# Attention by pairs of query tiles, with values and turned probabilities split into high and low parts

## The reference

```python
def block(args):                       # one tile of 128 queries
    qn, qp, i = args
    s = (jnp.einsum('bqhd,bkhd->bhqk', qn, k_nope)
         + jnp.einsum('bqhr,bkr->bhqk', qp, k_pe)).astype(jnp.float32) * scale
    s = jnp.where(causal, s, -jnp.inf)
    p = jax.nn.softmax(s, axis=-1).astype(v.dtype)
    return jnp.einsum('bhqk,bkhd->bqhd', p, v)
...
o_mla = mla_attention(...) * jax.nn.silu(g_mla)
o_s5 = s5_layer(...) * jax.nn.silu(g_s5)
return jnp.concatenate([o_mla, o_s5], axis=-1) @ w_out
```

## Time and profile before

| | us |
|---|---|
| median of 3 runs | 891.39 |
| the profiled execution | 895.35 |
| its span, from the first to the last instruction | 893.3 |
| TensorE busy (4360 matmuls) | 852.8, 95% |
| TensorE weight loads | 691.8, 77% |
| VectorE busy | 590.0, 66% |
| ScalarE busy | 326.9, 37% |
| GpSimd busy | 248.1, 28% |
| mean granted TensorE clock | 0.986 |

### The profile page before, as it was taken

How to read it: one execution, slowest core, us unless ns; L and a number is a source line. 1 busy time by engine, 2 the same in 40 slices (tenths; PEclk the granted TensorE clock), 3 DMA queues, 4 the chain that set the end, 5 groups by cost and what they waited for, 6 DMA issues and landing times.

```text
span 893.3 us, 12333 instructions
## 1 busy us (share of the span) xinstructions
PE 852.8 (95%) x4360; PEld 691.8 (77%) x4360; DVE 590.0 (66%) x961; ACT 326.9 (37%) x626; POOL 248.1 (28%) x251
## 2 busy tenths in 40 slices
PE   7999999999999999999998999999799999999995
PEld 5899777756677777787875888888588888888884
DVE  6988688557687775637871443488986667544543
ACT  6251514654333434412222645045243446111210
POOL 2000001415211111506656231005753013332243
PEclk9999999999999999999998899999999999999998
DMA  9101164220000111032223110236334322111111
GB/s 335 35 20 30 48 118 96 50 74 1 1 2 1 39 34 48 1 105 108 95 95 118 47 48 1 83 94 191 123 102 140 105 74 103 38 61 48 48 59 59
DMA packets 40685, 64.21 MB, mean 72 GB/s; under 512 B 8256, under 2 KB 21824, under 8 KB 40608
## 3 DMA queue, kind: packets, MB, share of 16 engines
q1 hardware_dynamic: 40624, 63.42, 23.2%
HBM read 52.33 MB, written 9.44 MB: 69 GB/s over the span
## 4 chain that ended last, share of the span: by engine, by line
PE 72%; DVE 17%; ACT 3%; DMA 3%; issue 2%; SPq 1%; POOL 1%; DVEq 0%; ACTq 0%; POOLq 0%
PE psum L1876 39%; PE psum L2177 14%; PE psum L2100 6%; PE psum L1963 6%; PE psum L1885 6%; PE psum L1911 1%; DVE vg_lo L1748 1%; DVE probT L696 1%; DMA wgs_raw<-even_w_in_dram 1%; DVE x_hi_raw L1779 1%; DVE x_lo_raw L1780 1%; DMA xT_raw<-x_cols_dram 1%; DMA ln_gb<-ln_b_dram 1%; DVE qTt L1617 1%; ACT xT_hi L1117 1%
## 5 line engine op out<-in xcount | busy, mean ns | idle before, releaser
L2177 PE MATMUL psum<-vg_hi,x1T_hi 128*128 128x512 f32 x208 | 82.0, 394 | 4.9 <-DVE vg_lo L1748 4.2
L2177 PE MATMUL psum<-vg_hi,x1T_lo 128*128 128x512 f32 x208 | 81.7, 393 | 0.0
L2177 PE MATMUL psum<-vg_lo,x1T_hi 128*128 128x512 f32 x208 | 81.6, 392 | 0.0
L2100 PEld LDWEIGHTS psum<-V,probT 128*128 128x128 f32 x576 | 69.3, 192 | 12.4 <-issue 8.4
L1209 ACT ACTIVATE prob<-psum,negmax 128x128 f32<-128x128 f32 (+7 forms) x64 | 47.4, 741 | 82.0 <-DVE negmax L1623 74.4
L2100 PE MATMUL psum<-V,probT 128*128 128x64 f32 x576 | 74.5, 275 | 0.5 <-DVE rot L1684 0.3
L1963 PE MATMUL psum<-kT,qTt 96*128 96x512 f32 (+3 forms) x192 | 72.5, 487 | 1.2 <-DVE YT L713 1.2
L1623 DVE TENSOR_REDUCE negmax<-psum 128x1 f32<-128x128 f32 (+7 forms) x64 | 48.5, 758 | 28.2 <-PE psum L1967 26.7
L696 DVE COPY probT<-psum 128x512 f32<-128x512 f32 (+3 forms) x64 | 37.8, 591 | 22.4 <-PE psum L1885 20.7
L2177 PEld LDWEIGHTS psum<-vg_hi,x1T_hi 128*128 128x128 f32 x208 | 39.3, 189 | 15.3 <-DVE vg_lo L1748 6.2
L1876 PE MATMUL psum<-x1T_lo,wqk_hi 128*128 128x512 f32 x128 | 50.8, 397 | 0.0
(11 more groups left out here) (393 smaller groups left out, 2087.5 us busy)
## 6 DMA issues: line engine op xcount, KB each, us to landing
vg_piece<-odd_w_in_dram SPq DMA_DIRECT2D x60, 256.0 KB, 3.3
wqk_raw<-odd_w_in_dram SPq DMA_DIRECT2D x8, 512.0 KB, 5.3
x_res<-x_dram SPq DMA_DIRECT2D x8, 512.0 KB, 4.0
x_scratch<-zn SPq DMA_DIRECT2D x8, 512.0 KB, 2.9
w_out_raw<-odd_w_out_dram SPq DMA_DIRECT2D x4, 1024.0 KB, 5.0
V<-x_scratch SPq DMA_DIRECT2D x8, 512.0 KB, 4.4
out_dram<-SG SPq DMA_DIRECT2D x8, 512.0 KB, 2.9
xT_raw<-x_cols_dram SPq DMA_DIRECT2D x7, 512.0 KB, 7.6
```

The lines of the kernel that those rows point to most:

```text
L2100: mm = pe.matmul(bank("o", i)[:, h * VD:(h + 1) * VD], lhsT, rhs, start=(k == 0), stop=(k == len(pairs) - 1))
L2177: mm = pe.matmul(bank(*job), lhsT, rhs, start=(k == 0 and j == 0 and product not in ADDS_TO), stop=(k == 3 and j == len(pairs) - 1), skip_ ...
```

## The change

- The 64 heads run in pairs of tiles: four pairs (2p, 2p+1), in each the 8 heads, and for each head the even and then the odd tile. Product "av" m belongs to the two heads 2m and 2m + 1.
- Values of a key block stand as four groups of 64 columns: for an even head high and low, for an odd head low and high (fp32r). ScalarE writes two copies, GpSimd subtracts.
- Turned probabilities go into one of three cells, each with a high and a low part (fp32r) for both tiles. ScalarE copies every group (high), VectorE subtracts this from the same bank (low).
- "av": the values (128 columns: high and low of one head) are stationary, the probabilities of both tiles (256 columns) move past them, once high and once low. In the last key block of a pair only the odd tile takes part. The output comes turned. Bank 7 holds two heads; when both are done, ScalarE copies it ("o" to `o_parts`), and two matmuls with a shifted identity ("ob") add the lower half onto the upper one or the reverse, in the same bank.
- The gate is scaled by the inverse row sums (`gate_scaled`), turned ("gT"), copied by ScalarE, and multiplied with the output by VectorE in two halves (`output_gated`). "OT" is gone.
- Queries of tiles 0 and 1 and the GLU product are done ahead of the first scores; the sigmoid is one function on ScalarE; the S5 gate is multiplied in four operations.
- w_out's rows are loaded and split after the last queries; `wqk`'s first load stands behind the last "o", ahead of the norm's rows, which wait for the last "ob"; its two splits stand behind the norm's tiles 2 and 3 on GpSimd.

The diff, cut to what the text speaks of (memory offsets and semaphore names left out):

```diff
...
+            yield "q", 1
-            yield "q", 1
+                yield "glu", n
+            yield "qT", 1
+            for n in range(4):
-            for n in range(4):
-                yield "glu", n
...
-        heads = [(i, h) for i in range(NT) for h in range(H)]
+        heads = [(2 * p + t, h) for p in range(NT // 2) for h in range(H) for t in range(2)]
...
+                p, r = divmod(n, 16)
-                if h < 2 and i + 1 < NT:
-                    yield "qT", (i + 1, h)
-                if h in (2, 3) and i + 2 < NT:
-                    yield "q", (i + 2, h - 2)
+                if p and r in (1, 2):
+                    yield "qT", (2 * p + r - 1, 1)
+                if p < 3 and r in (10, 11):
+                    yield "qT", (2 * p + r - 8, 0)
+                if p < 3 and r in ((3, 5, 6, 7) if p else (0, 1, 2, 3)):
+                    nth = ((3, 5, 6, 7) if p else (0, 1, 2, 3)).index(r)
+                    yield "q", (2 * p + 2 + nth // 2, nth % 2)
+                if n and n % 4 == 0:
+                    yield "gT", n // 4 - 1
-                if n:
-                    yield "av", n - 1
-                if h == 4 and i:
-                    yield "OT", i - 1
-            yield "av", len(heads) - 1
+                if n and n % 2 == 0:
+                    yield "av", n // 2 - 1
+                if n > 4 and n % 4 == 1:
+                    yield "ob", n // 4 - 1
+            yield "gT", STEPS // 2 - 1
+            yield "av", STEPS - 1
-            yield "OT", NT - 1
+            yield "ob", STEPS // 2 - 1
...
-        def values_done(engine, number):
-            n = next(n for n, key in enumerate(heads) if number in [j[0] for j in pt_jobs[key]])
-            i, h = heads[n]
-            if h == H - 1:
-                plan.filled(engine, ("o", i))
+        value_turns = {}
+        for m, g in cell_users:
+            if m % 2 == 0 or (m, g + 1) in cell_of:
+                value_turns[m, g] = len(value_turns) + 1
+        def values_done(engine, m, g):
+            if (m, g) in value_turns:
+                engine.wait_ge(pv_done, value_turns[m, g])
-                engine.wait_ge(pv_done, i * (H - 1) + h + 1)
-        def copy_probs(engine, step, number, first, blocks):
-            plan.filled(engine, ("pt", number))
-            if number >= 4:
-                values_done(engine, number - 4)
-            dst, src = probT[:, number % 4, 0:blocks * P], bank("pt", number)[:, 0:blocks * P]
-            ins = engine.activation(dst, src, ACT.Copy) if engine is nc.scalar else engine.tensor_copy(dst, src)
-            step.frees(ins, ("pt", number))
+                plan.filled(engine, ("o", m // 2))
+        def prob_blocks(n, number, first, blocks):
+            cell = cell_of[n // 2, first // 4]
+            source = bank("pt", number)[:, 0:blocks * P].rearrange("p (b t) -> p b t", b=blocks)
+            return [part[:, 0:blocks, n % 2, :] for part in cells[cell % 3]], source
...
+            for k in (1, 2):
+                w_out0_load(k, 0)
+            for k in (4, 5):
+                w_out0_load(k, 1)
-            wqk_load(0)
-            sp.wait_ge(s5_out_set, 16)
-            for k in range(4, 6):
-                w_out0_load(k, 2)
...
-                    sp.wait_ge(gated, NT)
+                    plan.filled(sp, ("o", STEPS // 2 - 1))
+                    wqk_load(0)
+                    plan.drained(sp, ("ob", STEPS // 2 - 1))
...
-                           q_turned)
-                if 2 <= i < 5:
-                    w_out0_split_slice(i - 1, 0, 48)
+                           *temps, q_turned)
+                for j in {1: range(0, 4), 3: range(4, NT)}.get(i, ()):
+                    plan.drained(pool, ("vp", j))
+                    step(pool.tensor_tensor(V[j][:, :, 1:3, :], V_raw[j][:, :, 1:3, :],
+                                            V[j][:, :, 0:4:3, :].bitcast(F32), ALU.subtract), values_split)
+            def wqk_split_part(h, part):
+                pool.wait_ge(wqk_loaded[h % 2], 32 * (h // 2 + 1))
+                split(*(t[:, 4 * part:4 * part + 4, :, :].rearrange("p k n c -> p k (n c)") for t in wqk[h % 2]),
...
+                pairs = bank("vp", i).rearrange("p (k s d) -> p k s d", k=H // 2, s=2)
+                step(act.activation(V[i][:, :, 0:4:3, :], pairs, ACT.Copy))
+                step.frees(act.activation(V_raw[i][:, :, 1:3, :], pairs, ACT.Copy), ("vp", i))
+                step.frees(act.activation(qt[n % 2][:, 4 * half:4 * half + 4, :],
+            for n in range(2):
+                scaled_queries(n, 0)
+                scaled_queries(n, 1)
...
+                step.frees(act.activation(SGL[:, k, :], bank(*job), ACT.Sigmoid, bias=gla_c[:, 6 + k // 2:7 + k // 2]),
+                           job)
+            for n in range(4):
+                exponentials(n)
+                plan.drained(act, ("ob", 4 * (i // 2) + 3))
+            def output_parts(j):
+                plan.filled(act, ("o", j))
+                step.frees(act.activation(o_parts[:, :], bank("o", j), ACT.Copy), ("o", j))
...
-                    for number, first, blocks in pt_jobs[heads[n]][1:]:
-                        copy_probs(act, step, number, first, blocks)
+                    if n > 4 and n % 4 == 1:
+                        output_parts(n // 4 - 1)
+                    if n == 2:
+                        act.wait_ge(s5_out_set, 4)
+                    for number, first, blocks in pt_jobs[heads[n]]:
+                        plan.filled(act, ("pt", number))
+                        cell = cell_of[n // 2, first // 4]
+                        if n % 2 == 0 and cell >= 3:
+                            values_done(act, *cell_users[cell - 3])
+                        (hi, _), source = prob_blocks(n, number, first, blocks)
+                        step(act.activation(hi, source, ACT.Copy), prob_hi_set)
+                elif what == "gT":
+                    plan.filled(act, ("gT", n))
+                    if n >= 2:
+                        plan.drained(act, ("ob", n - 2))
+                    step.frees(act.activation(gateT[n % 2][:, :], bank("gT", n)[:, 0:2 * P], ACT.Copy), ("gT", n))
+            output_parts(STEPS // 2 - 1)
...
+            step(vec.tensor_copy(shift[:, 0:VD], ident[:, VD:2 * VD]))
+            step(vec.tensor_copy(shift[:, 2 * VD:3 * VD], ident[:, 0:VD]))
+            step(vec.tensor_tensor(shift[:, VD:2 * VD], ident[:, 0:VD], ident[:, 0:VD], ALU.subtract))
+            queries_turned(1, 0)
+            queries_turned(1, 1)
+            for n in range(4):
+                score_max(n)
+            for k in range(4):
+                m, n = k // 2, k % 2
+                s = slice(n * 512, (n + 1) * 512)
+                plan.drained(vec, ("glu", m, n))
+                step(vec.tensor_tensor(gs5[:, m, s], gs5[:, m, s], SGL[:, k, :], ALU.mult), s5_out_set)
+            def gate_scaled(j):
+                p, k = divmod(j, 4)
+                plan.drained(vec, ("s", 4 * j + 3))
+                sums, inverses = (t[:, :, 2 * k:2 * k + 2] for t in (rsum, rinv))
+                step(vec.reciprocal(inverses, sums))
+                block_ = gate[:, k, 2 * p * P:2 * (p + 1) * P].rearrange("p (t h d) -> p t h d", t=2, h=2)
+                step(vec.tensor_tensor(block_, block_, inverses.unsqueeze(3).to_broadcast([P, 2, 2, VD]), ALU.mult),
+                     gated)
+            def output_gated(j):
+                p, k = divmod(j, 4)
+                plan.filled(vec, ("ob", j))
+                plan.drained(vec, ("gT", j))
+                cols = slice(2 * p * P, 2 * (p + 1) * P)
+                src = bank("ob", j)
+                step(vec.tensor_tensor(OT[0:VD, k, cols], src[0:VD, 0:2 * P], gateT[j % 2][0:VD, :], ALU.mult))
+                step.frees(vec.tensor_tensor(OT[VD:P, k, cols], src[VD:P, 2 * P:4 * P], gateT[j % 2][VD:P, :],
+                                             ALU.mult), ("ob", j))
...
+                    for number, first, blocks in pt_jobs[heads[n]]:
+                        vec.wait_ge(prob_hi_set, number + 1)
+                        (hi, lo), source = prob_blocks(n, number, first, blocks)
+                        step.frees(vec.tensor_tensor(lo, source, hi.bitcast(F32), ALU.subtract), ("pt", number))
+                    if n % 4 == 3:
+                        gate_scaled(n // 4)
+                elif what == "ob":
+                    output_gated(n)
...
+                    p, h = divmod(n, H)
+                        pe.wait_ge(values_split, 2 * p + 2)
+                    if h % 2 == 0:
+                        plan.claim(pe, ("o", n // 2))
+                    c0 = h % 2 * 2 * P
+                    for k in range(2 * p + 2):
+                        if k % 4 == 0:
+                            for key in heads[2 * n:2 * n + 2]:
+                                plan.drained(pe, ("pt", pt_jobs[key][k // 4][0]))
+                        t0 = int(k == 2 * p + 1)
```

(32 more changed lines are left out.)

118 lines of the change are left out of this document (43 added, 75 removed).

## The result

The changed kernel takes 940.1 us (median of 4 runs, 936.0 to 941.2), the kernel before 892.07 beside it: ratio 1.051 (1.0485 to 1.0534). The forecast was 918.3 with a range of 900 to 934: slower, as forecast, and 6 us beyond the range. The profiled execution has 941.18 us and a span of 939.5, 46.2 more than the span before.

The account below looks back on a forecast made before the run. TensorE, busy 95% of the span, was taken to bound the kernel. Start +3.1, early pairs +1.2 and -3.8, late heads with the end +26.4 gave +26.9 us: 922.2 profiled, 918.3 median, range 900 to 934.

Parts of the forecast that it names:

- The mechanism: Late heads (32 to 63): engines wait on each other in one serial round per head, so TensorE's saving is lost there.
- the first sign named: Profile after the change: ScalarE's exponentials wait for VectorE's maxima in nearly every late head; no size given.
- TensorE's saving: Product of probabilities and values: fewer matmuls, 64.5 us before, 37.8 plus 3.8 after, so 22.9 us less TensorE work.
- The ring: Heads 32 to 63: exponential, high copy, low parts, maximum in series; 68.4 us for the third pair, 76.6 for the fourth.
- The end: Last exponential to first product with w_out: last copies, low part, gates and product, 7.9 us where before 7.3.
- Early heads: First two pairs of tiles: no ring, but a wait at bank 7; 28 and 39 us for 26.8 and 42.8.
- The start: Up to the first turning: GLU product ahead of the first scores delays it from 193.1 to some 196.2 us, +3.1.
- S5's products behind as cover: Value copies on ScalarE, taken as two of 256 columns: hidden behind S5's TensorE products, costed at nothing; 1.4 us without cover.
- Behind the first product with w_out: After attention: norm rows load later behind the last gated output but land about when used, 0 to 2 us.
- Rival 2: Late heads: TensorE's idle gaps make the granted clock fall on top of the ring; +8 us, 926; 13%.
- Rival 1: Late heads: TensorE stays the bound because maxima get ahead and the ring doesn't hold; 872 us; 11%.
- rival 3: Late heads: VectorE's low part is cheaper than its priced row, 31 x 0.4 us less; 906 us; 5%.

Follow-up runs that it names:

- e6: Changed kernel with four cells for turned probabilities instead of three, low part written over the high part (output not the reference's): 934.4 us.
- e1: Changed kernel, from head 31 on ScalarE issues the high copies of a head ahead of the next head's exponentials: 926.5 us.
- e5: e1 with four cells for turned probabilities instead of three, low part written over the high part (output not the reference's): 907.4 us.
- e7: e1, and from head 34 on TensorE issues the last pair of heads' product ahead of the scores of head n+2: 908.5 us.
- e3: Changed kernel without VectorE's low parts of the turned probabilities; the products read the high part twice: 880.7 us.
- e9: Changed kernel, first product of each four heads (heads 0 to 31) and the turning of scaled gates (all heads) one head later: 936.5 us.
- e4: Changed kernel with the first four scores and their exponentials ahead of the GLU product again: 938.8 us.
- e12: Changed kernel with the late-head orders of e7, the delays of e9 and the start order of e4: 899.1 us.
- e11: Changed kernel with the late-head orders of e7 and the delays of e9, without ScalarE's second copy of the values (output not the reference's): 899.4 us.
- e2: Changed kernel, from head 30 on VectorE takes the maximum of head n+2 ahead of the low parts of head n: 951.6 us.

## Why the prediction was right and where it fell short

**The step that failed** is in the sum. It prices what the engines do and the order in which they wait, and gives no time to what is held until its last reader. The three cells and the gate turning had no term, bank 7 had none at the end, and the second copy of the values stood at nothing. In their place the runs show 5.0 us for the cells (e6), 4.4 in the early heads, 3.5 at the end and 3.5 at the start.

**The mechanism was right.** TensorE loses its work and waits; low parts wait for high copies 82.6 us; products pass 0.12 us apart. That exponentials wait for maxima in 32 waits was the first sign named, and a poor one, since the kernel before had it too. Undoing the order and the hold on cells (e1, e5, e7) brings most of it back, while the work stays.

**TensorE's saving was right in size**: 22.9 us forecast. e3 has 110.8 + 56.8 us busy where the kernel before has 125.3 + 63.7, 21.4 less. By four passes for an fp32 product (the Trainium skill, FP8 and Floating Point Precision, TensorE Precision Notes) nothing would have been gained; these runs go by the row of 0.224 us for two small matmuls, not by passes.

**The ring was right to 0.4 us, and the term that it lacked was the cells.** e6 without cell waits has 68.8 and 76.6 us where the sum had 68.4 and 76.6, and its single rounds agree too, so this is not luck; the changed kernel has 71.0 and 79.4. I had the three cells in the code and gave their wait no term: +2.2 and +2.8.

**The end**, 7.9 forecast, 11.4 measured. The first of its products waited 2.81 us for the last gated output at bank 7, which I had priced for the early heads alone, and in that wait the clock fell; its instructions pass 0.21 us apart instead of 0.12:

```profile
421.06 0.58 PE L2159 MATMUL psum<-probT_hi,V 128*128 128x256 f32 x1 [2.81 <-DVE gate L1716]
421.44 0.41 PE L2159 MATMUL psum<-probT_lo,V 128*128 128x256 f32 x1
421.65 0.41 PE L2159 MATMUL psum<-probT_hi,V 128*128 128x256 f32 x1
...
420.00:425.00 5.00, 3.94 (x19) 3.94 (x20) 2.19 (x5) 2.29 (x4) 0.00 (x0) 0.50 0.00 0
```

These 5 us are wholly at 1.2 GHz. The turning of the last head stands behind this product and starts at 424.53, 4.4 us after exp(63), where before the change it was 2.8. No run separates the wait from the clock.

**Early heads**, 67 forecast, 71.4 measured. "Up to 1.4 us, four times in each pair" was the right wait for bank 7 (five in all, 4.8 us together, the longest 1.5), but the gate turning, which stands ahead of the scores, had no term: it waited four times, 4.3 us together, twice for the scaled gate and twice for VectorE's copy of turned queries. e9 takes both kinds out and has 68.1 from first turning to turning(32), 1.1 us over the forecast.

**The start**, +3.1 forecast, +6.6 measured. From the turning of S5's outputs (184.84 us, before 181.72) to the first turning are 14.9 us for 11.4 before: the GLU order, priced at 3.1. Setting that order back brought the first turning 2.2 us (e4) and 1.9 us (e12) forward, so that much of the 3.5 is shown. The 3.1 ahead of that are the value copies, costed at nothing under "S5's products behind as cover" with 256 columns each. They have 512, so ScalarE's four copies take 2.51 us a tile (the three of before 1.88) and TensorE's products 1.72. From 160 us on TensorE's products follow at ScalarE's pace, 1.25 us for 0.86. What failed is the size, and the cover with it (my own price without cover was 1.4); e11 takes one copy out and gets its first turning 3.1 us earlier.

**Behind the first product with w_out**, 0 to 2 for the norm rows. 507.9 for 505.1 here, 503.5 to 504.3 in e1, e2, e3, e5, e6 and e7 with the same end: the rows cost nothing that can be told, and the 2.8 seem to be this execution's.

**Rival 2, the clock, came in part.** The late heads ran at 0.94. Exp(49) to exp(56), with two falls (0.69 at 345 to 350 us, 0.66 at 365 to 370), takes 37.3 us, less 1.4 for two query copies and 2.8 for two output groups 4.73 a round; exp(56) to exp(62), at 1.00, takes 30.7, less 2.3 for the mix and 1.4 for one group 4.50. The 1.6 us between them look like the price of the falls, but the waits of high copies for products differ as well, 345.7 to 383 us first, then 383 to 413.7:

```profile
ACT probT_hi L1281 <- PE psum L2159: 3.4, 4, 1.7
...
ACT probT_hi L1281 <- PE psum L2159: 0.4, 1, 0.4
```

In e6, with four cells and a fall of its own (0.79 at 362 to 370 us), exp(49) to exp(56) takes 34.9. So the 1.6 us are part of the 2.8 of the cells. Whether the slower clock lengthened the products for which the copies waited is not shown, since no run changes the clock alone; it is open how much of the 8 us of this rival came. TensorE was busy 79% of the late heads (128.0 of 161.6) and not the 70 to 75% of the forecast, partly for this slower clock. Rival 1 (872) and rival 3 (906) didn't come.

Together the missed terms in the profiled executions are 3.5 (start) + 4.4 (early heads) + 5.0 (cells) + 3.5 (end) + 2.8 (this execution's last part), 19.2 of the 19.3 us missed: all of one sign. My bounds allowed +11 for hand-overs, which were right (0.08 to 0.09), and nothing for resources that are held. Added up, the bounds reach 939 (918.3 + 11 + 5 + 5), 1 us short of the result, while the range stopped at 934; had it gone so far, it would nearly have been right for other reasons than the true ones. By the medians the miss is 21.8 us: I took off 4.0 because the profiled execution before lay above its median, and the one after lies only 1.1 above.

## What to carry to other kernels

Count, for each buffer and bank that a change shares, who must let go of it before the next write, and put that wait in the sum as a term of its own; then ask which instruction stands behind the waiter. Two limits in one loop hide each other: taking away either gave 6 and 14 us, both 33, so a single repair that gains little doesn't acquit its cause. And read the width of a new operation off its access pattern, since a copy "in two halves" may be two copies of the whole.

## What the runs showed of the hardware

Product instructions with 256 moving columns pass 0.12 us apart (389.03, 389.15, 389.27, 389.38), and the last ones with 128 columns 0.06 (390.58, 390.64). At a granted clock of 0.50 those with 256 are 0.21 apart (421.44, 421.65).

A granted clock below 1.00 followed idle times of 1.37 and 1.46 us in e4 (first two rows), and didn't follow ones of 1.48 and 1.35 us at nearly the same place in the changed kernel (last two; its clock is 1.00 from 200 to 228 us): a gap of this length makes a fall possible, not certain.

```profile
207.72 0.44 PE L1941 MATMUL psum<-ident,gate 128*128 128x128 f32 x2 [1.37 <-DVE gate L1705]
212.13 0.39 PE L2159 MATMUL psum<-probT_hi,V 128*128 128x256 f32 x1 [1.46 <-DVE gate L1716]
...
213.69 0.39 PE L2159 MATMUL psum<-probT_hi,V 128*128 128x256 f32 x1 [1.48 <-DVE gate L1716]
216.56 0.44 PE L1941 MATMUL psum<-ident,gate 128*128 128x128 f32 x2 [1.35 <-DVE gate L1705]
```
